# A two-block network on one core: state-space decay tiles as single-pass matmuls, and the split weights at another address

## What is computed

```python
cs = jnp.moveaxis(jnp.cumsum(da, axis=2), 2, -1)
tri = jnp.tril(jnp.ones((SSD_CHUNK, SSD_CHUNK), dtype=bool))
decay_in = jnp.exp(jnp.where(tri, cs[..., :, None] - cs[..., None, :], -jnp.inf))
cb = jnp.einsum('bclgn,bcsgn->bcgls', cc, bc)
scores = cb[:, :, :, None] * decay_in
y_diag = jnp.einsum('bcgels,bcsgep->bclgep', scores, xdt)
...
y_off = jnp.einsum('bclgn,bcgepn->bclgep', cc, entering) * state_decay[..., None]
```

## Time and profile before

| | |
|---|---|
| median of 3 runs | 2178.51 us (2171.35, 2178.51, 2179.12) |
| profiled execution, its own time | 2198.38 us |
| its span, first to last instruction | 2196.7 us |
| mean granted TensorE clock | 0.953 of full |
| PE busy | 2014.2 us (92%), 16141 matmuls |
| DVE busy | 1338.7 us (61%) |
| ACT busy | 1009.7 us (46%) |
| DMA | 334.00 MB, mean 152 GB/s |

### The profile page before, as it was taken

How to read it: one execution, slowest core, us unless ns; L and a number is a source line. 1 busy time by engine, 2 the same in 40 slices (tenths; PEclk the granted TensorE clock), 3 DMA queues, 4 the chain that set the end, 5 groups by cost and what they waited for, 6 DMA issues and landing times.

```text
span 2196.7 us, 39857 instructions
## 1 busy us (share of the span) xinstructions
PE 2014.2 (92%) x16141; PEld 1905.8 (87%) x16141; DVE 1338.7 (61%) x2015; ACT 1009.7 (46%) x1486; POOL 17.2 (1%) x36
## 2 busy tenths in 40 slices
PE   6999889999986799999799999889989898988998
PEld 5988879999875699999689888889988898887998
DVE  5834666666675666767567655555555765555554
ACT  5632455555458455555465510344445552024443
POOL 0000000000000000000000000000000000000000
PEclk9997999999998999999899999989999999998999
DMA  7520336666633266666234300235443340022553
GB/s 282 189 98 1 118 145 260 258 259 258 251 116 120 96 238 260 257 258 229 79 132 154 135 1 1 98 134 185 180 171 115 128 161 20 1 77 100 196 195 124
DMA packets 43886, 334.00 MB, mean 152 GB/s; under 512 B 4864, under 2 KB 4992, under 8 KB 5504
## 3 DMA queue, kind: packets, MB, share of 16 engines
q1 hardware_dynamic: 38592, 277.89, 34.5%
q0 software_dynamic: 4608, 50.33, 6.1%
q10 hardware_dynamic: 576, 4.19, 0.5%
HBM read 331.35 MB, written 1.05 MB: 151 GB/s over the span
## 4 chain that ended last, share of the span: by engine, by line
PE 84%; DVE 9%; ACT 4%; issue 2%; DMA 1%; DVEq 0%; ACTq 0%
PE unit L479 14%; PE unit L480 14%; PE unit L481 14%; PE acc L479 7%; PE acc L480 7%; PE acc L481 7%; PE acc L1756 2%; PE misc L1296 2%; PE unit L1749 2%; PE misc L375 2%; PE misc L1760 2%; ACT w_hi L456 1%; DVE w_lo L463 1%; PE unit L622 1%; PE unit L619 1%
## 5 line engine op out<-in xcount | busy, mean ns | idle before, releaser
L463 DVE TENSOR_TENSOR w_lo<-raw,w_hi 128x1024 fp32r<-128x1024 f32 x526 | 640.1, 1224 | 490.8 <-ACT w_hi L456 480.7
L456 ACT ACTIVATE w_hi<-raw 128x1024 fp32r<-128x1024 f32 x526 | 554.8, 1060 | 683.5 <-PE unit L481 409.4
L479 PE MATMUL unit<-h_hi,w_hi 128*128 128x256 f32 x2656 | 756.9, 285 | 49.9 <-DVE h_lo L390 33.0
L480 PE MATMUL unit<-h_lo,w_hi 128*128 128x256 f32 x2656 | 749.2, 282 | 0.0
L481 PE MATMUL unit<-h_hi,w_lo 128*128 128x256 f32 x2656 | 748.9, 282 | 0.0
L479 PEld LDWEIGHTS unit<-h_hi,w_hi 128*128 128x128 f32 x2656 | 512.2, 193 | 59.9 <-issue 41.4
L480 PEld LDWEIGHTS unit<-h_lo,w_hi 128*128 128x128 f32 x2656 | 509.3, 192 | 0.2
L481 PEld LDWEIGHTS unit<-h_hi,w_lo 128*128 128x128 f32 x2656 | 509.3, 192 | 0.0
L479 PE MATMUL acc<-mv_hi,w_hi 128*128 128x256 f32 x1360 | 387.2, 285 | 36.6 <-DVE mv_lo L535 36.6
L480 PE MATMUL acc<-mv_lo,w_hi 128*128 128x256 f32 x1360 | 382.9, 282 | 0.0
L481 PE MATMUL acc<-mv_hi,w_lo 128*128 128x256 f32 x1360 | 382.5, 281 | 0.0
(11 more groups left out here) (304 smaller groups left out, 2098.8 us busy)
## 6 DMA issues: line engine op xcount, KB each, us to landing
raw<-w_in SPq DMA_DIRECT2D x263, 1024.0 KB, 4.8
ada_ring<-ada_in POOLq DMA_DIRECT2D x32, 1536.0 KB, 8.4
con<-con_in ACTq DMA_DIRECT2D x1, 1424.0 KB, 6.2
keep<-gates_in ACTq DMA_DIRECT2D x1, 1280.0 KB, 5.6
par<-par_in ACTq DMA_DIRECT2D x1, 1261.0 KB, 14.8
x<-x_in SPq DMA_DIRECT2D x1, 1024.0 KB, 5.9
out<-x SPq DMA_DIRECT2D x4, 256.0 KB, 2.3
con<-con_in ACTq DMA_DIRECT2D x1, 130.0 KB, 6.1
```

The source lines that it names most:

```text
L456: act(half(w_hi, c, k), raw[c % RAW][:, CW // 2 * k:CW // 2 * (k + 1)], ACT.Copy).then_inc(S("high_parts"), 1)
L463: tt(half(w_lo, c, k), raw[c % RAW][:, CW // 2 * k:CW // 2 * (k + 1)], half(w_hi, c, k).bitcast(f32), ALU.subtract).then_inc(S("chunk_spli ...
L479: mm(out, w, m, start=first, stop=False)
L480: mm(out, w, ml, start=False, stop=False)
```

## The change

Two things are done.

**The decay tiles.** Behind the five transposes between the 12 and the 8 units, four new float32 matmuls copy `r_cs` of both chunks to four blocks of 32 partitions in `misc1`: chunk 0 twice, chunk 1 twice. ACT makes float32r copies of the matrix `fold` (the 32 columns of an identity repeated four times down the partitions), of the identity and of the mask, and rounds the four blocks into `cs_parts`. DVE replaces the second block of each chunk by what the rounding left, so that `cs_parts` holds high and low parts of each chunk on 64 neighbouring partitions. A half of `decays` is then four float32r matmuls over 64 partitions that add the two parts (L625 of the changed kernel), and one of 512 columns (L627) that adds the mask to all four heads at once. PE's wait for the rest of the constants moves to ACT, and in its place PE waits for `cs_parts`. `dt_in` and `dt_cs` become two counts of one semaphore.

**The addresses.** The four new tensors take 1,664 bytes of each partition, and an unused tensor of 192 bytes is put behind `keep`. Together that is 7 x 256 + 64 bytes, so that `w_hi` and `w_lo` (and `late`) start at 0 modulo 256 instead of 192. `h_hi`, `h_lo`, `mv_hi` and `mv_lo` stay at 128; `keep` moves from 192 to 64.

```diff
@@ -292,12 +292,17 @@
         rstd = sb("rstd", [P, T])
         tmp = sb("tmp", [P, 4, T])
         cact = sb("cact", [P, 8])
+        fold_r = sb("fold_r", [P, 32], f32r)
+        ident_r = sb("ident_r", [P, P], f32r)
+        neg_up_r = sb("neg_up_r", [P, P], f32r)
+        cs_parts = sb("cs_parts", [P, P], f32r)
         mod2 = sb("mod", [P, 2, 48])
         gsc2 = sb("gsc", [P, 2, 16])
 
 
         keep_cols, late_cols = 10752, 10240
         keep = sb("keep", [P, keep_cols])
+        sb("weights_offset", [P, 48])
         with nc.sbuf_tensor("late", [P, late_cols], f32) as late:
             pass
         w_hi = [sb(f"w_hi{i}", [P, CW], f32r) for i in range(2)]
@@ -614,13 +619,14 @@
                     b = unit[m % 2]
                     if m < 2:
                         pe.wait_ge(S("unit_free"), 22)
+                    rows = slice(64 * c, 64 * (c + 1))
                     for k in range(4):
                         hd = 8 * g + 4 * half + k
-                        mm(b[:, P * k:P * (k + 1)], ident[0:HR, hd:hd + 1].to_broadcast([HR, P]),
-                           r_cs[:, P * c:P * (c + 1)], start=(k == 0), stop=False, skip_group_check=True)
-                    for k in range(4):
-                        ins = mm(b[:, P * k:P * (k + 1)], ident, cn("neg_up"), start=False, stop=(k == 3),
-                                 skip_group_check=True)
+                        ins = mm(b[:, P * k:P * (k + 1)], fold_r[rows, hd:hd + 1].to_broadcast([64, P]),
+                                 cs_parts[rows, :], start=(k == 0), stop=False, skip_group_check=True)
+                    ins = mm(b[:, :].rearrange("p (a n) -> p a n", a=4), ident_r[:, :],
+                             neg_up_r[:, :].unsqueeze(1).to_broadcast([P, 4, P]), start=False, stop=True,
+                             skip_group_check=True)
                     ins.then_inc(S("ssd_decay_ps"), 1)
 
 
@@ -636,10 +642,14 @@
             pe.wait_ge(S("ssd_rows"), 1)
             for n, (src, c) in enumerate(((r_dt, 0), (r_dt, 1), (r_ncs, 0), (r_ncs, 1), (r_dtd, 0))):
                 ins = nc.tensor.transpose(misc[1][:, 32 * n:32 * (n + 1)], src[:, P * c:P * (c + 1)], ident[0:HR, 0:HR])
+            for q in range(4):
+                c = q // 2
+                ins = mm(misc[1][32 * q:32 * (q + 1), 256:384], ident[0:HR, 0:HR], r_cs[:, P * c:P * (c + 1)],
+                   start=True, stop=True, skip_group_check=True)
             ins.then_inc(S("ssd_tok_ps"), 1)
             pe_units(pe, CH0["ssd_in"] + 12, U0["ssd_in"] + 12, 8)
 
-            pe.wait_ge(S("con_rest"), 16)
+            pe.wait_ge(S("ssd_rows"), 2)
             pe.wait_ge(S("ssd_conv_done"), 24)
             for g in range(4):
                 ins = nc.tensor.transpose(bank(0, P * g, P * (g + 1)), xbc[:, 16 + g, 0:P], ident)
@@ -719,12 +729,12 @@
         def act_ssd(ac, link):
 
             ac.preload_act_table_set(LN_EXP)
-            ac.wait_ge(S("dt_in"), 1)
+            ac.wait_ge(S("dt_steps"), 1)
             link(act(r_a, r_dt, ACT.Abs))
             link(act(r_b, r_a, ACT.Exp, scale=-1.0))
             link(act(r_b, r_b, ACT.Ln, bias=one("one", HR)))
             act(r_one[:, 0:1], pr("a_log", 0, HR), ACT.Exp).then_inc(S("dt_log"), 1)
-            ac.wait_ge(S("dt_cs"), 1)
+            ac.wait_ge(S("dt_steps"), 2)
 
             link(act(r_dtd, r_cs, ACT.Exp, bias=r_cs[:, P - 1:P], scale=-1.0))
             act(r_ncs, r_cs, ACT.Copy, scale=-1.0)
@@ -755,6 +765,11 @@
 
             ac.wait_ge(S("unit_free"), 12 + 2)
             ac.wait_ge(S("ssd_tok_ps"), 1)
+            ac.wait_ge(S("con_rest"), 16)
+            act(fold_r[:, :], cn("fold", 0, 32), ACT.Copy)
+            act(ident_r[:, :], ident, ACT.Copy)
+            act(neg_up_r[:, :], cn("neg_up"), ACT.Copy)
+            act(cs_parts[:, :], misc[1][:, 256:384], ACT.Copy).then_inc(S("dt_decays"), 1)
             for n in range(8):
                 ahead(act_split, ac, 12 + n)
                 done_after(ac, 12 + n)
@@ -820,7 +835,7 @@
         def dve_ssd(dve, link):
 
             dve.wait_ge(S("dt_raw"), 1)
-            ts(r_dt, misc[1][0:HR, 0:T], pr("dt_bias", 0, HR), None, ALU.add).then_inc(S("dt_in"), 1)
+            ts(r_dt, misc[1][0:HR, 0:T], pr("dt_bias", 0, HR), None, ALU.add).then_inc(S("dt_steps"), 1)
             dve.wait_ge(S("dt_log"), 1)
             link(stt(r_dt, r_dt, 0.0, r_b, ALU.max, ALU.add))
             link(ts(r_da, r_dt, r_one[:, 0:1], -1.0, ALU.mult, ALU.mult))
@@ -828,7 +843,7 @@
             for c in range(2):
                 s = slice(P * c, P * (c + 1))
                 ins = nc.vector.tensor_tensor_scan(r_cs[:, s], r_one[:, s], r_da[:, s], 0.0, ALU.mult, ALU.add)
-            ins.then_inc(S("dt_cs"), 1)
+            ins.then_inc(S("dt_steps"), 1)
             dve.wait_ge(S("dt_decays"), 1)
             tt(r_dtd, r_dtd, r_dt, ALU.mult).then_inc(S("ssd_rows"), 1)
             conv = A["conv"]
@@ -852,6 +867,13 @@
                 dve.sem_inc(S("unit_free"), 1)
             for n in range(8):
                 ahead(dve_split, dve, 12 + n)
+                if n == 1:
+
+                    dve.wait_ge(S("dt_decays"), 2)
+                    for p in (32, 96):
+                        v = cs_parts[p:p + 32, :]
+                        ins = tt(v, misc[1][p:p + 32, 256:384], v.bitcast(f32), ALU.subtract)
+                    ins.then_inc(S("ssd_rows"), 1)
             done_after(dve, 19)
             dve.wait_ge(S("ssd_tok_ps"), 1)
             nc.vector.tensor_copy(tokv, misc[1][:, 0:160]).then_inc(S("ssd_tok"), 1)
```

## The result

| | before | changed |
|---|---|---|
| median, in the same session | 2174.93 us (4 runs, 2164.85 to 2179.12) | 2211.18 us (4 runs, 2210.98 to 2212.14) |
| ratio, with its 95% interval | | 1.0149 (1.011 to 1.0188) |
| profiled execution, its own time | 2198.38 us | 2211.30 us |
| mean granted clock | 0.953 | 0.953 |
| matmul records | 16141 | 15973 |

The changed kernel is 36 us slower; 20 faster had been forecast, and it lies outside the range. Medians and ranges are of all executions, while the ratios leave out those over 1.5% above the fastest of the same kernel, so that a ratio is not quite the quotient of the two medians.

The account below looks back on a forecast made before the run. PE was taken to bound the kernel, with 84% of the chain. Decay tiles gain 19.9 us and the addresses 0: 2198.4 - 19.9 = 2178.5 for the profiled execution, 2178.5 - 19.9 = 2158.6, so 2159 us for the median; range 2095 to 2185.

Parts of the forecast that it names:

- What bounds the kernel: Whole kernel: PE is 84% of the chain of waits, so a change counts by what it takes from PE.
- Part 2, "I take 0": Split matmuls: moving the weights' address leaves both paces as they are, 0 us; bounds 96 gained, 55 lost.
- Part 1: Scan: the new decay tiles gain 19.9 us (19.5 + 0.9 - 0.5), from 12 to 31 by clock.
- 4 x 115.6 = 0.46 us: Decay tiles: PE time of a half at full clock, against 2.17 before, from the pace of 256-column matmuls.
- a sign of being wrong: Scan, chunk 0: the prediction is wrong if PE is still the chain there; DVE's 5.06 us loop was expected.
- +0.9: Scan, chunk 1: us gained, the middle of +8.7 at full clock and -7 at half clock.
- 2178.5 - 19.9: Last step: the scan gain taken from the median of the runs, giving 2158.6, so 2159 us.
- The additions: Four new float32 matmuls on PE cost 0.5 us, at most 0.9; the added ACT and DVE work mostly covered.
- Rival A: Split matmuls: the lower pace (113.3 ns) everywhere, 28 us more gained, 2131, up to 2150; chance 0.24.
- B: Split matmuls: no stall at all, 108 ns each, 96 us more gained, 2063; chance 0.13.
- C: Split matmuls: the stall grows with operand distance, 120.0 ns, 55 us lost, 2214; chance 0.11.
- D: Scan: the clock stays at half through both chunks, decay tiles then worth 12 us, 2167; chance 0.10.

Follow-up runs that it names:

- eight places: The changed kernel with the split weights at each 32-byte step modulo 256 from the split activations: 2168.8 us (64 above) to 2223.0 us (0).
- the addresses alone: The kernel before with 64 bytes put ahead of the split weights and the old decay tiles kept: 2217.7 us, ratio 1.0187.
- the first profile and the second: Two profiled executions of the unchanged kernel before: 2198.38 us, then 2163.85 us when it was measured again beside the experiments.

## Why the prediction was wrong

- **What bounds the kernel:** right. Both parts showed as PE time, one as pace and one in the scan.
- **Part 2, "I take 0":** this step failed, and with it the forecast. The addresses cost 42 us, with the new tiles (2211.2 against 2168.8) as with the old (2217.7 against 2175.3). The argument was that the pace changed with the address fixed, and stayed in the exchanged units, so something besides the address set it. The first is true (851 and 885 in the same stage of two executions), but it only shows that the address is not all. From the exchanged units I concluded that the sign brings nothing better, and so that the address does nothing; the second does not follow from the first. The sign does count: 64 above has both paces, 115.5 ns in the mean, and 64 below nearly the upper, 117.8 ns, alone (851 in both windows of the kernel with the weights at 64, distance 192), 117.7. The row alone could not have told: in three later profiles with the distances of before, one of the two exchanged stretches runs at 113.3 ns.
- **The Trainium skill's rule** that loading weights takes no read bandwidth from the running matmul (page "TensorE: Matmul & The Clock Gate", Part 2, step 1) would leave all eight places equal. They lie between 115.5 and 119.9 ns. That the two reads meet is the reading that fits the distance and the half clock (213.3 ns, nothing lost); a direct look at what they meet at is not in these runs.
- **Part 1 at the profile:** 24 us where 19.9 stood, by two errors of opposite sign. "4 x 115.6 = 0.46 us" for a half was wrong in both of its parts. The four matmuls of 128 columns take 0.59 us and the one of 512 takes 0.43, where half of 0.46 had been taken for each; at half clock they take 1.04 and 0.72. Matmuls of 128 columns start 112 ns apart at full clock and 213 at half, no faster than those of 256. What holds the one of 512 columns was not tried. So at half clock PE stayed the chain of chunk 0, which the prediction had named as a sign of being wrong: 5.44 us for a group and not 5.06 with DVE as the bound, and 17 us gained up to y(3) and not 19.5. On the other side chunk 1, for which I took +0.9 as the middle of two clocks, was at full clock from 188.7 on and gained 6 us of its own.
- **Part 1 at the median:** some 10 us (6.5 between the medians of the addresses alone and the changed kernel). The step that failed is the last: "2178.5 - 19.9". The gain was taken against a profile in which the scan ran at half clock for 34 us, and by the mean granted clocks most executions of the kernel before do not. The remark on the 19.9 us between profile and median named the pace; between the first profile and the second the clock of the scan has 17 of 34.5 us, and the pace some 6.5.
- **The additions:** right, 0.35 us for 0.5.
- **Rival A** (113.3 ns everywhere) and **B** (no stall): no place gives either. **C** had the sign, and nearly the number by luck: 120.0 ns where 118.8 was measured, and 19.9 us for part 1 where the medians give 6.5. Its law is wrong: 0 is the worst place, with 160. **D** (half clock in both chunks) was right for chunk 0 in all profiles without extra work and wrong for chunk 1.

## What to carry to other kernels

When a tensor is added or resized ahead of matmul operands, look at the distance of the two operands modulo 256 bytes, and count matmuls in a window of a dense stage before and after; here eight places spread over 4.4 ns of 115, 2.5% of the time, and the tiles' own 1,664 bytes, without any offset, cost 25 us. Before a saving read from one profile is set against a median, ask whether that profile's clock is the usual one: two profiles of the kernel before would have shown 17 us of the scan to be a matter of clock. And a shorter matmul is not a cheaper one for being short: read from a trace at what distance the shorter form starts.

## What the runs showed of the hardware

- Single-pass matmuls of 128x256, each with a weight load of its own, start every 115.5 to 119.9 ns in the mean at full clock, by how far the stationary operand lies above the moving one modulo 256 bytes; at half clock every 213.3 ns in all kernels.
- At some distances there are two paces (113.3 and 117.8 ns at 64), one of which lasts through a stream and changes only where it is interrupted, differently in each execution; at 0 there is one, 120.0.
- float32 matmuls did not change pace in any of these kernels: 112 ns a record of 128 columns by a stationary tile of 128 throughout.
- Single-pass matmuls of 128 columns (64 partitions, in groups of four) start no faster than those of 256: 112 ns. That the load of 128 weight columns takes this long would explain it; it was not tried apart. One pair of rows points that way: in float32, 16 records with a stationary tile of 64 columns take 1.02 us (L708), 64 ns each, and 8 with one of 128 take 0.89 (L692), 111 ns each; but the former start in pairs, so that it proves nothing.
- PE's clock fell to half during fully busy work of small matmuls behind a stretch with gaps, or did not, in executions of the same program (the old tiles, 0.50 and 1.00). With the new tiles it fell in all eleven profiles and in the one with the gaps ahead of them filled; it stayed at full in the one profile with PE's waits in chunk 0 filled as well.
